# S5 states laid out by step within a chunk, tokens reordered through the gated linear layer

## The chip, the cores and the metric

The kernel runs on one core of one Trainium2 chip. The metric is the device time of one execution in microseconds (us), as the median of several; smaller is better.

## The reference, cut to what matters

One layer of a hybrid decoder for 288 tokens: 256 of one prompt, and 8 sampled sequences of 4 tokens. After a norm, z = a @ w_in is split into an mLSTM part and a part u for the S5 part (64 groups of 16 channels, 64 complex states each). The S5 part is

```python
ab = exp(dt * A)                       # complex, one per group and state
bu = einsum('gpc,bsgc->bsgp', Bb, u)   # complex
st[t] = ab * st[t-1] + bu[t]           # along the tokens of each sequence
y  = einsum(C_re, st_re) - einsum(C_im, st_im) + D * u
ys = gelu(y)
ys = ys * sigmoid(ys @ w_glu + b_glu)  # the gated linear layer, per token
mix = concat(hm, ys) @ w_out
```

`hm` is the mLSTM part's result. The states at the last token of each sequence are outputs too. Behind it come a PEER feed-forward layer (routed experts) and a gated embedding, which the change doesn't touch. Everything is in 32 bits.

## The kernel before, in words

Activations lie with channels on the 128 partitions and the T = 288 tokens along the free dimension: tokens 0 to 255 are the prompt (TP), then sample token TP + 4 b + s for sequence b and step s. A large tile `work` holds, one behind the other, the S5 states `st` (real and imaginary part, each NJ = 32 tiles of 288), `zT` (32 tiles), `uT` (8 tiles), `mix` (16 tiles) and a scratch area. There are 8 PSUM banks `ps`.

Each engine has its own program; they are tied by counting semaphores, and each engine runs its instructions in the order written. The order of the work around the change is by hand:

1. PE, `pe_linear` (L246): the "u" linear, 8 tiles of 128 columns, 16 matmuls over k each, weights streamed by SP through the two halves of `ring`. ACT's `copy_tiles` (L1783, L1792) copies each tile from PSUM to `uT`. Then PE's gate rows (L1686).
2. ACT computes Exp and Sin (L1802 to L1804) for the discretised A; DVE's `dve_s5_setup` (L456, L492 to L514, then L518 to L534) makes the coefficients, and PE transposes them (L1691, L1696, L1712). `a` broadcast over tokens is a stride of 0 in the innermost dimension. L523 to L526 multiply B by such a broadcast; L531 writes runs of 16 with gaps of 16.
3. PE, L1723: the Bu products, 32 tiles x 2 (real, imaginary); ACT (L1816) and DVE (L1871) copy them to `st`.
4. PE goes on with the "z" linear: 32 tiles, 512 matmuls. Beside it DVE runs the S5 scan, `dve_s5_scan` (L563). The prompt is cut into 16 chunks (NCH) of 16 steps (CH). After four squarings of a (`cmul`, L550) come
   - the samples: 4 steps, each one `cmul_add` (L536) on 8 sequences x 32 tiles = 256 elements;
   - a first loop (L585) of 15 trips: step i + 1 of all 16 chunks at once, 32 x 16 = 512 elements a pass;
   - a middle loop (L591) of 15 trips along the chunks' last steps, 32 elements a pass;
   - a third loop (L602) of 15 trips: adds the carried state, times a power of a, to step i of chunks 1 to 15, 32 x 15 = 480 elements a pass, and a `cmul` of 32 elements for the next power.

   One `cmul_add` is 8 passes (L538 to L541, L543, L544, L546, L547); each reads or writes `st` and the contiguous scratch `tS`. In `st` the token is innermost, so step t of all chunks is every 16th element:

```python
chk = [s[:, :, 0:TP].rearrange("p j (k t) -> p t j k", t=CH) for s in st]
smp = [s[:, :, TP:T].rearrange("p j (b s) -> p s j b", s=NS) for s in st]
```

5. L609 to L614 copy the last states to `send` and release PE (`s5_ready`, `send_ready`). PE, L1735: the products of C with the states, 8 tiles u of 4 x 2 matmuls each over 32 columns, moving operand `st[q][:, 4*u+r, :]`. DVE adds D u (L1876), ACT takes Gelu (L1821), both in place in `uT`. PE then transposes the states (L1741, L1743) and broadcasts 8 gate rows (L1752, evacuated at L1828).
6. PE, the "glu" linear: 8 tiles of 8 matmuls, from `uT`. ACT takes the sigmoid of each from PSUM to `gel` (L1844, two buffers) and DVE multiplies by `uT` into `mix[8 + c]` (L1882). Before that DVE works out the mLSTM gate rows (L879 to L915).
7. The mLSTM part (L705 on; DVE L921 on), then the output projection, which reads `mix` split in two parts.

Only SP issues DMAs: the weights of "u", "z" and "glu" (L1591), each half of `ring` as soon as the block before in it is done, then S5 outputs, mLSTM states and w_out tiles.

Of the kernel before, what the change touches and what calls it, by code (L numbers as in the profile page):

```python
# [39 lines left out]
NJ = G * SP_ // P  # L40
CH = 16
NCH = TP // CH
PH, PK, TK = 8, 128, 16
UA = 36
PLE = 256
# [63 lines left out]
def build(nc, ins, outs):  # L109
    ctx = ExitStack()  # L110
    with ctx:
# [68 lines left out]

            return ap.unsqueeze(len(ap.shape)).to_broadcast([*ap.shape, n])

        st = [wk(O_RE, NJ, T), wk(O_IM, NJ, T)]
        zT = wk(O_Z, 32, T)
        uT = wk(O_U, 8, T)
        mix = wk(O_MIX, 16, T)
        xin = wk(O_Z, 3, D)

        Bn = [wk(0, NJ, GC), wk(512, NJ, GC)]
# [373 lines left out]
        def dve_s5_scan(v, o):  # L563
            o.settle()
            v.wait_ge(sem("s0_copied"), 1)
            a = [abT[:, 0, :], abT[:, 1, :]]
            pw = [a16[:, 0, :], a16[:, 1, :]]
            g2 = [a16[:, 2, :], a16[:, 3, :]]

            ts = [t[:, :, 0] for t in tS]  # L570
            cmul(v, o, pw, a, a, ts)
            for _ in range(3):
                cmul(v, o, pw, pw, pw, ts)

            smp = [s[:, :, TP:T].rearrange("p j (b s) -> p s j b", s=NS) for s in st]
            s0 = [s0T[:, q, :].rearrange("p (b j) -> p j b", j=NJ) for q in range(2)]
            aB = [bc(x, NB) for x in a]
            for s in range(NS):
                src = s0 if s == 0 else [x[:, s - 1] for x in smp]
                cmul_add(v, o, [x[:, s] for x in smp], aB, src, [t[:, :, 0:NB] for t in tS])  # L580

            chk = [s[:, :, 0:TP].rearrange("p j (k t) -> p t j k", t=CH) for s in st]
            aC = [bc(x, NCH).unsqueeze(1) for x in a]
            tC = [t.unsqueeze(1) for t in tS]
            with v.Fori(0, CH - 1) as i:  # L585
                o.loop(i, {"dve_own": CMUL})
                cmul_add(v, o, [x[:, ds(i + 1, 1)] for x in chk], aC, [x[:, ds(i, 1)] for x in chk], tC)
                o.leave(CH - 1)

            end = [s[:, :, CH - 1:TP:CH] for s in st]  # L590
            with v.Fori(0, NCH - 1) as i:  # L591
                o.loop(i, {"dve_own": CMUL})
                cmul_add(v, o, [x[:, :, ds(i + 1, 1)] for x in end], [x.unsqueeze(2) for x in pw],
                         [x[:, :, ds(i, 1)] for x in end], [t[:, :, 0:1] for t in tS])
                o.leave(NCH - 1)

            for q in range(2):
                o.do(v.tensor_copy(g2[q], a[q]))
            o.settle()
            n = NCH - 1  # L600
            prev = [x[:, :, 0:n].unsqueeze(1) for x in end]
            with v.Fori(0, CH - 1) as i:  # L602
                o.loop(i, {"dve_own": CMUL + 6})
                cmul_add(v, o, [x[:, ds(i, 1), :, 1:NCH] for x in chk], [bc(x, n).unsqueeze(1) for x in g2], prev,
                         [t[:, :, 0:n].unsqueeze(1) for t in tS])
                cmul(v, o, g2, g2, a, ts)
                o.leave(CH - 1)
            for q in range(2):
                o.do(v.tensor_copy(send[:, q, 0, :], st[q][:, :, TP - 1]))  # L609
                o.do(v.tensor_copy(send[:, q, 1:1 + NB, :],  # L610
                                   st[q][:, :, TP + NS - 1:T:NS].rearrange("p j b -> p b j")))
            o.settle()
            o.do(v.tensor_copy(g2[0], g2[0]), sem("s5_ready"))
            o.do(v.tensor_copy(g2[1], g2[1]), sem("send_ready"))  # L614
# [1047 lines left out]
        def _(pe):  # L1662
# [67 lines left out]
            for u in range(8):  # L1730
                if u >= 2:
                    pe.wait_ge(sem("y_sum"), u - 1)
                for r in range(4):
                    for q in range(2):
                        m = pe.matmul(ps[4 + u % 2][32 * r:32 * r + 32, 0:T], CT[q][:, u, 32 * r:32 * r + 32],  # L1735
                                      st[q][:, 4 * u + r, :], start=(q == 0), stop=(q == 1))
                m.then_inc(sem("y_done"), 1)

            pe.wait_ge(sem("send_ready"), 1)
# [25 lines left out]
        def _(act):  # L1765
# [30 lines left out]
                        one(i, b)  # L1796
                    o.leave(nb // 2)

            copy_tiles("u", uT)
            act.wait_ge(sem("theta_ready"), 1)  # L1800

            o.do(act.activation(r32[0:NJ, 4, :], r32[0:NJ, 2, :], ACT.Exp))  # L1802
# [10 lines left out]
                              ps[4 + g % 4][:, 0:512].rearrange("p (a b) -> p a b", b=P)), sem("bct_copied"))  # L1813
            for j in range(NJ):
                act.wait_ge(sem("bu_done"), 2 * j + 1)
                o.do(act.copy(st[0][:, j, :], ps[4 + 2 * (j % 2)][:, 0:T]), sem("bu_copied0"))  # L1816
            copy_tiles("z", zT)

            for u in range(8):
# [35 lines left out]
        @block.vector  # L1855
        def _(v):
            o = Own(v, sem("dve_own"))
            v.wait_ge(sem("const_ready"), 1)
            for g in range(1, 12, 2):
                i, q = divmod(g, 4)  # L1860
                t0, n = TOK[i]
                v.wait_ge(sem("xt_done"), g + 1)
                o.do(v.tensor_copy(hT[:, 4 * q:4 * q + 4, t0:t0 + n],
                                   ps[g % 4][:, 0:4 * n].rearrange("p (a b) -> p a b", b=n)), sem("xt_copied1"))
            v.wait_ge(sem("vec_copied"), 1)
            v.wait_ge(sem("xt_copied0"), 6)
            dve_norm(v, o, 0)
            dve_s5_setup(v, o)
            for j in range(NJ):
                v.wait_ge(sem("bu_done"), 2 * j + 2)  # L1870
                o.do(v.tensor_copy(st[1][:, j, :], ps[5 + 2 * (j % 2)][:, 0:T]), sem("bu_copied1"))  # L1871
            v.wait_ge(sem("bu_copied0"), NJ)
            dve_s5_scan(v, o)
            for u in range(8):
                v.wait_ge(sem("y_done"), u + 1)
                o.do(v.scalar_tensor_tensor(uT[:, u, :], uT[:, u, :], gv[:, 80 + u:81 + u], ps[4 + u % 2][:, 0:T],  # L1876
                                            ALU.mult, ALU.add), sem("y_sum"))
            dve_gate_rows(v, o)
            base = STREAM["glu"][0]
            for c in range(8):  # L1880
                v.wait_ge(sem("mm_freed"), 2 * base + c + 1)
                o.do(v.tensor_tensor(mix[:, 8 + c, :], uT[:, c, :], gel[:, c % 2, :], ALU.mult), sem("glu_ready"))  # L1882
            dve_mlstm(v, o)

            squares = dve_squares(v, 1, "tile_freed")

            def add(i, c, s):

                v.wait_ge(sem("q_used"), i * 8 + (4 * c + 4))
                h = low[:, ds(i * (2 * T) + c * T, T)]  # L1890
                o.do(v.tensor_tensor(h, h, ps[4 + s][:, 0:T], ALU.add), sem("tile_freed"))
                squares(i, c, s)

            low_parts(v, o, "out", None, add, {"tile_freed": 2}, ahead=True)
            o.settle()
            low_parts(v, o, "wq", None, None, {}, only_first=True)
            dve_norm(v, o, 1, ffn_h, ffn_l)
            dve_peer(v, o)
            dve_tail(v, o)
# [27 lines left out]
```

## Time and profile before

| | |
|---|---|
| time of the runs | median 3019.31 us of 3 (3018.59 to 3023.04) |
| span of the profiled execution, first to last instruction | 3016.9 us |
| its own time beside that | not given apart; the median of the runs lies 2.4 us above the span |
| mean granted TensorE clock | 0.956 |
| share of the span busy | PE 94%, PEld 88%, DVE 57%, ACT 40%, POOL 0% |
| the chain that ended last | PE 78%, DVE 14%, issue 4%, ACT 2% |
| DMA | 389 MB, mean 129 GB/s |

The span is that of one profiled execution. PE is the matmul side of TensorE and PEld its weight loads, which overlap; DVE is VectorE, ACT ScalarE, POOL GpSimd, SP the engine that issues DMAs. A group of instructions is named by its line, engine and operation, with output and inputs by tile names; "idle before" is the time for which its engine stood still just ahead of it, with what ended that. An fp32 matmul has two records. The granted clock is given as a share of 2.4 GHz: 1.00, or 0.50 for 1.2 GHz.

### The profile page before, as it was taken

The page shows a single profiled execution, that of the slowest core. Times are in us where ns is not written, and L with a number is a line of the kernel's source. Part 1 is how long each engine was busy: PE and PEld are TensorE (multiplying, and loading weights), DVE is VectorE, ACT ScalarE, POOL GpSimd, SP SyncE. Part 2 cuts the span into 40 slices and gives each one's busy share as a digit, 9 for nine tenths or more (in the row PEclk, how much of TensorE's full clock was granted, in tenths as well). Part 3 has the DMA queues.
Part 4 walks back from the last instruction along what each step waited for, and adds up shares of the span by engine and source line. Part 5 has one row for each costly group of instructions (what it writes and reads, how often), then busy time and mean ns, then how long its engine had stood idle before and what let it go on. Part 6 is the DMA issues. An engine that isn't in the chain of part 4 may idle for free.

```text
span 3016.9 us, 53624 instructions
## 1 busy us (share of the span) xinstructions
PE 2834.0 (94%) x19564; PEld 2661.5 (88%) x19564; DVE 1717.4 (57%) x3311; ACT 1213.0 (40%) x2023; POOL 2.5 (0%) x18
## 2 busy tenths in 40 slices
PE   8999946899899998799999999999999999999997
PEld 6677734669799997699999999999999999999887
DVE  2289895566658887933333333335555555555466
ACT  1200002213344446944444444444444444444443
POOL 0000000000000000000000000000000000000000
PEclk9799977779899999999999999999999999999999
DMA  6124412226543331033333333344445544444543
GB/s 163 56 91 132 139 56 86 87 84 182 157 133 125 125 129 66 0 125 127 137 125 126 136 127 125 132 151 166 166 167 167 164 155 162 162 166 166 171 112 115
DMA packets 218075, 389.29 MB, mean 129 GB/s; under 512 B 21348, under 2 KB 167396, under 8 KB 200676
## 3 DMA queue, kind: packets, MB, share of 16 engines
q1 hardware_dynamic: 218020, 388.56, 39.0%
q8 instruction: 34, 0.56, 0.1%
q14 instruction: 21, 0.17, 0.0%
HBM read 374.04 MB, written 14.49 MB: 129 GB/s over the span
## 4 chain that ended last, share of the span: by engine, by line
PE 78%; DVE 14%; issue 4%; ACT 2%; DVEq 1%; DMA 0%; ACTq 0%
PE ps L389 11%; PE ps L390 11%; PE ps L391 11%; PE ps L1182 9%; PE ps L1185 9%; PE ps L1181 9%; PE ps L1113 7%; PE ps L261 3%; PE ps L812 1%; PE ps L1723 1%; DVE work L544 1%; DVE work L547 1%; DVE work L539 1%; DVE work L540 1%; DVE work L541 1%
## 5 line engine op out<-in xcount | busy, mean ns | idle before, releaser
L389 PE MATMUL ps<-ffn_h,part_h 128*128 128x288 f32 x2176 | 685.8, 315 | 14.8 <-issue 10.3
L390 PE MATMUL ps<-ffn_l,part_h 128*128 128x288 f32 x2176 | 642.3, 295 | 0.0
L391 PE MATMUL ps<-ffn_h,part_l 128*128 128x288 f32 x2176 | 639.1, 294 | 0.0
L1181 PE MATMUL ps<-act_h,v_high 128*128 128x288 f32 x2048 | 551.8, 295 | 6.1 <-DVE act_l L1418 3.6
L1182 PE MATMUL ps<-act_l,v_high 128*128 128x288 f32 x2048 | 552.2, 295 | 0.0
L1421 DVE TENSOR_TENSOR v_low<-ring,v_high 128x1024 fp32r<-128x1024 f32 x256 | 313.8, 1226 | 372.1 <-ACT v_high L1292 372.1
L1214 ACT CAST part_h<-ps 128x512 fp32r<-128x512 f32 x512 | 299.7, 586 | 466.1 <-PE ps L1113 465.4
L445 DVE TENSOR_TENSOR part_l<-ps,part_h 128x512 fp32r<-128x512 f32 x368 | 254.0, 691 | 404.9 <-ACT part_h L1214 402.4
L389 PEld LDWEIGHTS ps<-ffn_h,part_h 128*128 128x128 f32 x2176 | 409.8, 188 | 18.0 <-issue 16.2
L390 PEld LDWEIGHTS ps<-ffn_l,part_h 128*128 128x128 f32 x2176 | 412.0, 189 | 0.0
L391 PEld LDWEIGHTS ps<-ffn_h,part_l 128*128 128x128 f32 x2176 | 409.7, 188 | 0.0
L1292 ACT CAST v_high<-ring 128x1024 fp32r<-128x1024 f32 x256 | 268.5, 1049 | 346.0 <-PE ps L1185 346.0
L1181 PEld LDWEIGHTS ps<-act_h,v_high 128*128 128x128 f32 x2048 | 384.8, 188 | 6.5 <-DVE low L1433 3.8
L1182 PEld LDWEIGHTS ps<-act_l,v_high 128*128 128x128 f32 x2048 | 385.5, 188 | 0.0
L261 PE MATMUL ps<-low,ring 128*128 128x288 f32 x1280 | 315.8, 411 | 6.5 <-DVE low L308 6.5
L1185 PE MATMUL ps<-act_h,v_low 128*128 128x288 f32 x2048 | 314.3, 295 | 0.0
L261 PEld LDWEIGHTS ps<-low,ring 128*128 128x128 f32 x1280 | 246.2, 193 | 76.4 <-issue 7.7
L1113 PE MATMUL ps<-ident,ring 128*128 128x128 f32 x2048 | 305.9, 272 | 2.0 <-ACT work L1206 1.1
L1185 PEld LDWEIGHTS ps<-act_h,v_low 128*128 128x128 f32 x2048 | 287.0, 188 | 0.0
L1113 PEld LDWEIGHTS ps<-ident,ring 128*128 128x128 f32 x2048 | 250.6, 141 | 2.5 <-ACT work L1206 1.4
L445 DVE TENSOR_TENSOR part_l<-ring,part_h 128x512 fp32r<-128x512 f32 x160 | 108.3, 690 | 95.0 <-ACT part_h L429 94.6
L429 ACT CAST part_h<-ring 128x512 fp32r<-128x512 f32 x160 | 98.4, 620 | 144.5 <-PE ps L391 138.8
(339 smaller groups left out, 3212.2 us busy)
## 6 DMA issues: line engine op xcount, KB each, us to landing
ring<-in_peer_u SPq DMA_DIRECT2D x128, 1024.0 KB, 5.3
ring<-in_peer_v SPq DMA_DIRECT2D x128, 1024.0 KB, 5.6
ring<-in_w_in SPq DMA_DIRECT2D x20, 2048.0 KB, 8.0
ring<-in_w_out SPq DMA_DIRECT2D x16, 1024.0 KB, 5.9
ring<-in_w_ple_gate SPq DMA_DIRECT2D x16, 1024.0 KB, 5.9
out<-work SPq DMA_DIRECT2D x37, 256.0 KB, 3.2
work<-in_state_mlstm_C SPq DMA_DIRECT2D x32, 256.0 KB, 4.9
ring<-in_peer_w_q SPq DMA_DIRECT2D x8, 1024.0 KB, 5.7
```

The costliest lines, as they stand in the source:

```text
L261: m = pe.matmul(ps[2 * s + c][:, 0:T], ring[:, s, k * WB + c * P:k * WB + (c + 1) * P], rhs[:, k, :], start=(k == 0), stop=(k == kt - 1))
L389: pe.matmul(bank, w_h, rhs_h, start=start, stop=False)
L390: pe.matmul(bank, w_h, rhs_l, start=False, stop=False)
L391: return pe.matmul(bank, w_l, rhs_h, start=False, stop=stop)
L445: o.do(v.tensor_tensor(part_l[:, q, :], src, part_h[:, q, :].bitcast(F32), ALU.subtract), sem("low_done"))
L1113: m = pe.transpose(ps[q][:, j * P:(j + 1) * P], natural[s][:, k * P:(k + 1) * P], ident[:])
L1181: pe.matmul(ps[c][:, 0:T], w_h, a_h, start=st_, stop=False)
L1182: pe.matmul(ps[c][:, 0:T], w_h, a_l, start=False, stop=False)
L1185: m = pe.matmul(ps[c][:, 0:T], vl[:, s, c * P:(c + 1) * P], a_h, start=False, stop=sp_)
L1214: o.do(act.copy(part_h[:, q, :], ps[q][:, 0:512]), sem("high_done"))
L1292: o.do(act.copy(vh[:, s % 2, :], natural[s // 2][:, 1024 * (s % 2):1024 * (s % 2) + 1024]), sem("vh_done"))
L1421: o.do(v.tensor_tensor(vl[:, s % 2, :], natural[s // 2][:, 1024 * (s % 2):1024 * (s % 2) + 1024], vh[:, s % 2, :].bitcast(F32), ALU.subtra ...
```

## The change

A new constant CW = 16 + 32/16 = 18 is the number of tokens of one step. `st` becomes (step i of 16, tile j of 32, c of 18): for step i and tile j first the 16 chunks' token of that step, then 2 sample tokens (sample step s and sequence pair m have i = 4 s + m, c = 16 + b mod 2). All of one step's rows now lie in one stretch of 32 x 18 elements, and 16 chunks are neighbours. Neither size nor place of any tile changes.

The tokens of `uT` are put in the order (i, c) too, when ACT copies the u tiles from PSUM: two copies a tile instead of one (prompt, samples), written out instead of looped. They stay in it through Bu, the y products, Gelu and the glu linear, which work per token. L1882's product puts them back in order while it writes `mix`, in two passes a tile instead of one. The Bu copies (L1816, L1871), the passes of the scan, the copies to `send` and L1735's moving operand use the new layout; counts of semaphores, DMAs and matmuls stay.

```diff
--- before.py
+++ after.py
@@ -40,6 +40,7 @@
 NJ = G * SP_ // P
 CH = 16
 NCH = TP // CH
+CW = NCH + NS * NB // CH
 PH, PK, TK = 8, 128, 16
 UA = 36
 PLE = 256
@@ -180,10 +181,21 @@
 
             return ap.unsqueeze(len(ap.shape)).to_broadcast([*ap.shape, n])
 
-        st = [wk(O_RE, NJ, T), wk(O_IM, NJ, T)]
+        st = [work[:, O_RE + q * (O_IM - O_RE):O_RE + q * (O_IM - O_RE) + NJ * T].rearrange("p (i j c) -> p i j c", i=CH, c=CW) for q in range(2)]
         zT = wk(O_Z, 32, T)
         uT = wk(O_U, 8, T)
         mix = wk(O_MIX, 16, T)
+
+        def by_step(ap):
+
+            both = ap.rearrange("p (i c) -> p i c", c=CW)
+            return both[:, :, 0:NCH], both[:, :, NCH:CW].rearrange("p (s m) c -> p s m c", s=NS)
+
+        def by_token(ap):
+
+            return (ap[:, 0:TP].rearrange("p (k i) -> p i k", i=CH),
+                    ap[:, TP:T].rearrange("p (m c s) -> p s m c", s=NS, c=CW - NCH))
+
         xin = wk(O_Z, 3, D)
 
         Bn = [wk(0, NJ, GC), wk(512, NJ, GC)]
@@ -572,14 +584,16 @@
             for _ in range(3):
                 cmul(v, o, pw, pw, pw, ts)
 
-            smp = [s[:, :, TP:T].rearrange("p j (b s) -> p s j b", s=NS) for s in st]
-            s0 = [s0T[:, q, :].rearrange("p (b j) -> p j b", j=NJ) for q in range(2)]
-            aB = [bc(x, NB) for x in a]
+            W2 = CW - NCH
+            smp = [x[:, :, :, NCH:CW].rearrange("p (s m) j c -> p s m j c", s=NS) for x in st]
+            s0 = [s0T[:, q, :].rearrange("p (m c j) -> p m j c", j=NJ, c=W2) for q in range(2)]
+            aB = [bc(x, W2).unsqueeze(1).to_broadcast([P, NB // W2, NJ, W2]) for x in a]
+            tW = [t.rearrange("p j c -> p (j c)")[:, 0:NB * NJ].rearrange("p (m j c) -> p m j c", j=NJ, c=W2) for t in tS]
             for s in range(NS):
                 src = s0 if s == 0 else [x[:, s - 1] for x in smp]
-                cmul_add(v, o, [x[:, s] for x in smp], aB, src, [t[:, :, 0:NB] for t in tS])
-
-            chk = [s[:, :, 0:TP].rearrange("p j (k t) -> p t j k", t=CH) for s in st]
+                cmul_add(v, o, [x[:, s] for x in smp], aB, src, tW)
+
+            chk = [x[:, :, :, 0:NCH] for x in st]
             aC = [bc(x, NCH).unsqueeze(1) for x in a]
             tC = [t.unsqueeze(1) for t in tS]
             with v.Fori(0, CH - 1) as i:
@@ -587,7 +601,7 @@
                 cmul_add(v, o, [x[:, ds(i + 1, 1)] for x in chk], aC, [x[:, ds(i, 1)] for x in chk], tC)
                 o.leave(CH - 1)
 
-            end = [s[:, :, CH - 1:TP:CH] for s in st]
+            end = [x[:, CH - 1, :, 0:NCH] for x in st]
             with v.Fori(0, NCH - 1) as i:
                 o.loop(i, {"dve_own": CMUL})
                 cmul_add(v, o, [x[:, :, ds(i + 1, 1)] for x in end], [x.unsqueeze(2) for x in pw],
@@ -606,9 +620,8 @@
                 cmul(v, o, g2, g2, a, ts)
                 o.leave(CH - 1)
             for q in range(2):
-                o.do(v.tensor_copy(send[:, q, 0, :], st[q][:, :, TP - 1]))
-                o.do(v.tensor_copy(send[:, q, 1:1 + NB, :],
-                                   st[q][:, :, TP + NS - 1:T:NS].rearrange("p j b -> p b j")))
+                o.do(v.tensor_copy(send[:, q, 0, :], st[q][:, CH - 1, :, NCH - 1]))
+                o.do(v.tensor_copy(send[:, q, 1:1 + NB, :].rearrange("p (m c) j -> p m j c", c=W2), smp[q][:, NS - 1]))
             o.settle()
             o.do(v.tensor_copy(g2[0], g2[0]), sem("s5_ready"))
             o.do(v.tensor_copy(g2[1], g2[1]), sem("send_ready"))
@@ -1733,7 +1746,7 @@
                 for r in range(4):
                     for q in range(2):
                         m = pe.matmul(ps[4 + u % 2][32 * r:32 * r + 32, 0:T], CT[q][:, u, 32 * r:32 * r + 32],
-                                      st[q][:, 4 * u + r, :], start=(q == 0), stop=(q == 1))
+                                      st[q][:, :, 4 * u + r, :], start=(q == 0), stop=(q == 1))
                 m.then_inc(sem("y_done"), 1)
 
             pe.wait_ge(sem("send_ready"), 1)
@@ -1796,7 +1809,10 @@
                         one(i, b)
                     o.leave(nb // 2)
 
-            copy_tiles("u", uT)
+            for b in range(8):
+                act.wait_ge(sem("mm_done"), 2 * STREAM["u"][0] + b + 1)
+                for x, (d, e) in enumerate(zip(by_step(uT[:, b, :]), by_token(ps[b % 4][:, 0:T]))):
+                    o.do(act.copy(d, e), sem("mm_freed") if x else None)
             act.wait_ge(sem("theta_ready"), 1)
 
             o.do(act.activation(r32[0:NJ, 4, :], r32[0:NJ, 2, :], ACT.Exp))
@@ -1813,7 +1829,8 @@
                               ps[4 + g % 4][:, 0:512].rearrange("p (a b) -> p a b", b=P)), sem("bct_copied"))
             for j in range(NJ):
                 act.wait_ge(sem("bu_done"), 2 * j + 1)
-                o.do(act.copy(st[0][:, j, :], ps[4 + 2 * (j % 2)][:, 0:T]), sem("bu_copied0"))
+                o.do(act.copy(st[0][:, :, j, :], ps[4 + 2 * (j % 2)][:, 0:T].rearrange("p (i c) -> p i c", c=CW)),
+                     sem("bu_copied0"))
             copy_tiles("z", zT)
 
             for u in range(8):
@@ -1868,7 +1885,8 @@
             dve_s5_setup(v, o)
             for j in range(NJ):
                 v.wait_ge(sem("bu_done"), 2 * j + 2)
-                o.do(v.tensor_copy(st[1][:, j, :], ps[5 + 2 * (j % 2)][:, 0:T]), sem("bu_copied1"))
+                o.do(v.tensor_copy(st[1][:, :, j, :], ps[5 + 2 * (j % 2)][:, 0:T].rearrange("p (i c) -> p i c", c=CW)),
+                     sem("bu_copied1"))
             v.wait_ge(sem("bu_copied0"), NJ)
             dve_s5_scan(v, o)
             for u in range(8):
@@ -1879,7 +1897,9 @@
             base = STREAM["glu"][0]
             for c in range(8):
                 v.wait_ge(sem("mm_freed"), 2 * base + c + 1)
-                o.do(v.tensor_tensor(mix[:, 8 + c, :], uT[:, c, :], gel[:, c % 2, :], ALU.mult), sem("glu_ready"))
+                parts = zip(by_token(mix[:, 8 + c, :]), by_step(uT[:, c, :]), by_step(gel[:, c % 2, :]))
+                for x, (d, y, w) in enumerate(parts):
+                    o.do(v.tensor_tensor(d, y, w, ALU.mult), sem("glu_ready") if x else None)
             dve_mlstm(v, o)
 
             squares = dve_squares(v, 1, "tile_freed")
```

## Rows read from the trace of the kernel before

**Rows 1.** The page, part 1: busy us (share of the span) xinstructions

```profile
PE 2834.0 (94%) x19564; PEld 2661.5 (88%) x19564; DVE 1717.4 (57%) x3311; ACT 1213.0 (40%) x2023; POOL 2.5 (0%) x18
```

**Rows 2.** Waits of PE, 90 to 560 us: in total, times, longest

```profile
PE ps L1735 <- DVE work L613: 64.6, 1, 64.6
PE ps L1712 <- DVE ex L534: 5.6, 1, 5.6
```

**Rows 3.** Timeline: start us, us, engine, line, operation, [idle <-releaser]

```profile
403.71 5.74 PE L261 MATMUL ps<-low,ring 128*128 128x288 f32 x23
...
409.62 0.37 SPq L1591 DMA_DIRECT2D ring<-in_w_glu  x1
...
473.85 0.18 DVE L613 COPY work<-work 128x32 f32<-128x32 f32 x1
...
474.09 9.74 PE L1735 MATMUL ps<-work 128*32 128x288 f32 x128 [64.63 <-DVE work L613]
```

**Rows 4.** Timeline of DVE where the scan begins

```profile
159.05 0.21 DVE L552 TENSOR_TENSOR work<-work 128x32 f32<-128x32 f32 x1 [0.20 <-DVE work L1871]
```

**Rows 5.** Groups of DVE by shape: busy, mean ns; first loop of the scan

```profile
L546 DVE TENSOR_TENSOR work<-work 128x512 f32 x15 | 16.0, 1068 | 0.5
...
L539 DVE TENSOR_TENSOR work<-work 128x512 f32<-128x512 f32 x15 | 15.3, 1019 | 0.0
```

**Rows 6.** The same view, third loop of the scan

```profile
L546 DVE TENSOR_TENSOR work<-work 128x480 f32 x15 | 15.2, 1010 | 0.5
...
L539 DVE TENSOR_TENSOR work<-work 128x480 f32<-128x480 f32 x15 | 14.5, 967 | 0.0
```

**Rows 7.** The same view, passes over other layouts

```profile
L1882 DVE TENSOR_TENSOR work<-work,gel 128x288 f32<-128x288 f32 x8 | 3.5, 454 | 10.7 <-ACT gel L1844 10.7
...
L531 DVE TENSOR_TENSOR work<-work 64x512 f32<-64x512 f32 x4 | 2.7, 687 | 0.1
...
L546 DVE TENSOR_TENSOR work<-work 128x256 f32<-128x256 f32 x4 | 2.5, 628 | 0.1
...
L523 DVE TENSOR_TENSOR work<-work 128x512 f32<-128x512 f32 x1 | 0.7, 692 | 0.1
```

**Rows 8.** The same view, middle loop of the scan

```profile
L538 DVE TENSOR_TENSOR work<-work 128x32 f32<-128x32 f32 x15 | 3.3, 218 | 6.5 <-DVE work L547 6.5
```

**Rows 9.** Timeline from the last u copy to PE's L1691

```profile
93.88 0.40 ACT L1792 COPY work<-ps 128x288 f32 x1 [7.36 <-PE ps L261]
...
96.32 0.28 DVE L492 TENSOR_TENSOR work<-work 32x128 f32<-32x128 f32 x1 [55.53 <-ACT work L1804]
...
101.53 0.32 PEld L1691 LDWEIGHTS ps<-ident,work 32*128 32x128 f32 x4 [0.48 <-DVE work L514]
```

**Rows 10.** Groups by shape: copies from PSUM by ACT and DVE

```profile
L1871 DVE COPY work<-ps 128x288 f32<-128x288 f32 x32 | 14.5, 457 | 36.3 <-PE ps L1723 36.3
L1816 ACT COPY work<-ps 128x288 f32<-128x288 f32 x32 | 12.7, 398 | 30.7 <-PE ps L1723 30.4
...
L1812 ACT COPY work<-ps 128x512 f32<-128x512 f32 x8 | 4.4, 593 | 7.0 <-PE ps L1712 7.0
```

**Rows 11.** Timeline: two successive DVE L1876 behind L1735

```profile
480.96 0.52 DVE L1876 SCALAR_TENSOR_TENSOR work<-work,gv,ps 128x288 f32<-128x288 f32 x1 [0.46 <-PE ps L1735]
...
481.93 0.52 DVE L1876 SCALAR_TENSOR_TENSOR work<-work,gv,ps 128x288 f32<-128x288 f32 x1 [0.46 <-PE ps L1735]
```

**Rows 12.** Windows: us, busy by engine, PE clock, DMA share, GB/s

```profile
380.00:409.00 29.00, 29.00 (x121) 22.75 (x120) 27.08 (x46) 1.19 (x3) 0.00 (x0) 1.00 0.32 107
...
474.00:475.00 1.00, 0.91 (x8) 0.45 (x12) 0.11 (x2) 0.00 (x0) 0.00 (x0) 0.50 0.00 0
480.00:482.00 2.00, 2.00 (x40) 1.47 (x36) 1.09 (x3) 0.90 (x3) 0.00 (x0) 1.00 0.00 0
...
492.00:498.00 6.00, 6.00 (x13) 4.21 (x13) 0.00 (x0) 5.59 (x6) 0.00 (x0) 0.50 0.01 3
```

**Rows 13.** Timeline of DVE behind the last glu product

```profile
545.48 0.17 DVE L921 COPY ex<-ps 128x8 f32<-128x8 f32 x1 [18.10 <-PE ps L728]
```

## The prediction

> **What bounds the kernel now.** I read the page first, then the waits of PE, then the seam that the waits point at, in the timeline. PE is busy for 2834.0 of the 3016.9 us of the span [rows 1], so a change on another engine can only pay where PE stands still for it. Between 90 and 560 us the waits of PE hold one such place: L1735, the product of CT with the S5 states, waits 64.6 us for DVE L613; the next largest wait is 5.6 us [rows 2]. The timeline shows the seam. The last group of the "z" linear starts at 403.71 and lasts 5.74 us, so PE is done at 409.45; DVE is then in the last of its three loops and releases PE only with L613, which starts at 473.85; L1735 begins at 474.09, after 64.63 us of idle PE [rows 3]. The scan started at 159.05 with L552 [rows 4], right behind the last Bu copy, and z behind the last Bu product. So two chains start together near 159 us: PE's z linear, some 250 us, and DVE's scan, 315 us. The scan ends last by 64.6 us, and that is all the change can win from the scan: past it, PE's z linear ends the stage.
>
> Why are the passes of the scan so long? The first loop (L587) runs 15 trips of 8 passes over 128x512, the third (L604) 15 trips of 8 over 128x480. The means of the eight 512 passes lie between 1019 and 1068 ns (the cheapest and the dearest are shown) [rows 5], those of the eight 480 passes between 967 and 1010 ns [rows 6]. The same engine, operation and number of elements takes 692 ns in L523, which also has one operand broadcast along the inner 16, and 687 ns in L531, whose inner runs are 16 elements with gaps between them; 288 elements in L1882 take 454 ns [rows 7]. What L538 to L547 have and these rows lack is an inner step of 16 tokens (64 B). The sample passes, with an inner step of 4 tokens, take 628 ns for 256 elements [rows 7]. From 454 and 692 ns, a contiguous element costs 238/224 = 1.06 ns, so 480 elements cost 692 - 32 x 1.06 = 658 ns and 256 cost 420 ns.
>
> **The change part by part.**
> *Scan loops.* The change gives each step i of the chunk its own block of 32 rows, each of 18 consecutive tokens-by-chunk; a pass reads 16 (or 15) neighbours of each row. I take the contiguous price, since L531's runs of 16 with gaps are nearest in shape. The first loop's passes take (1019 + 1068)/2 = 1044 ns in the middle [rows 5], so 8 x (1044 - 692) = 2.8 us are saved a trip, 42.2 us in 15. The third loop's take 989 ns [rows 6]: 8 x (989 - 658) = 2.65 us a trip, 39.7 us in 15. Together 81.9 us. The bounds: the upper is this; the lower is nothing, if rows at a pitch of 72 B behave like the 64 B steps of today. The middle loop (15 trips of 8 passes of 32 elements) and the cmul of the third loop touch single elements before and after, only at other pitches: L538 at 32 elements takes 218 ns with a pitch of 1152 B, L552 takes 0.21 us with 64 B [rows 4, 8]. So nothing.
> *Sample passes.* 32 passes of 256 elements now have pairs of neighbours in the inner dimension. Between 628 ns (nothing saved) and 420 ns (6.7 us saved) I take nothing; the scan ends early enough either way.
> The scan then ends at 474.1 - 81.9 = 392.2 us, 17 us before PE is done at 409.45 [rows 3]. The wait of 64.6 us goes whole as soon as 64.6/240 = 0.27 us a pass is won of the 0.34 (81.9/240) that I expect. What is late next is PE's own z linear, which the change doesn't touch. **Term: -64.6 us.**
> *u copies on ACT.* Eight copies of 128x288 (0.40 us) become sixteen: 256 elements read at steps of 64 B from PSUM, and 32. Seven of the eight pairs lie beside PE, with some 7 us of idle ACT before each, as before the last (7.36). The last doesn't lie beside it: it starts at 93.88, ACT's Exp and Sin follow, they release DVE L492 at 96.32, DVE's chain ends with L514, and PE L1691 at 101.53 waited its last 0.48 us for that [rows 9]. So what the last pair costs more shifts all of it, z and scan alike. From ACT's 398 ns at 288 and 593 at 512 [rows 10], 0.87 ns an element: 256 cost 370, 32 cost 175, and back to back some 0.1 us overlaps: 0.45 against 0.40, the lower bound +0.05. With DVE's excess of (1040 - 692)/512 = 0.68 ns an element for the step it is 0.62, +0.22; twice that excess gives the upper bound, +0.40. **Term: +0.2 us.**
> Here ACT reads PSUM in steps, which no row of before does. The Trainium skill (SBUF — State Buffer, the paragraph on cachelines) says that PSUM lines hold two fp32 values and that non-contiguous PSUM access slows matmuls; by that rule the copy too should be slower and the term lie nearer to +0.4 than to +0.05. The same paragraph says that an SBUF line is 16 bytes and wants two hits: the 628 ns of the 16 B step [rows 7] agree, and by it the pairs of the sample passes would be at full rate, the scan ending at 385.5 us instead of 392.2. Neither is needed for the sum.
> *Bu copies (L1816, L1871).* 64 copies now write rows of 18 with gaps. They take 398 and 457 ns and wait for PE (30.7 and 36.3 us in total) [rows 10]; PE sets this stage. At nothing; if each rose by a half, still covered, but for the last, +0.2.
> *y matmuls (L1735).* The moving operand becomes 16 rows of 18 instead of 288 in a row. No row of before shows PE reading so. Bounds: nothing, or DVE's ratio 1040/692 = 1.5 on the steady pace of 0.97 us a tile (from one L1876 to the next [rows 11]), 8 x 0.49 = +3.9. I take nothing, since runs of 18 are nearer to L531's than to steps.
> *The clock of L1735.* After the idle stretch the granted clock is 0.50 (the 1.2 GHz level), and is still so at 474 to 475; from 480 on it is 1.00 [rows 12]. The eight tiles take from 474.09 to 483.83; at the steady pace they take 7.8 us. Without the idle stretch PE enters at 1.00 (380 to 409 us shows it) [rows 12]. **Term: -1.9 us.** The clock is down again at 0.50 in 492 to 498, in the first glu tiles, behind the thin broadcasts of L1752 [rows 12]; I keep that as it is. If it doesn't fall, up to 3 us more are won (the 6 us from 492 to 498 at twice the rate); if it falls already as L1735 begins, up to 7.8 are lost.
> *glu products (L1882).* Eight of 454 ns become sixteen: 256 elements written in steps (0.42 to 0.63) and 32 (0.21). At most +0.4 each. The earlier ones lie beside PE's glu tiles, with 10.7 us of idle DVE before them [rows 7]; after the last, DVE idles 18.10 us before L921 [rows 13]. At nothing; were that cover gone, 8 x 0.4 = 3.2 us.
> *Copies to send (L609, L610), waits.* Four copies ahead of L613, in DVE's slack. No DMA is added or moved. SP's glu load of 409.62 starts when z is done [rows 3]; L1735 and L1752 lie before its use, as now. No wait is added; behind L613 nothing stands now that is due before z's end.
>
> **Sum** against the profiled execution: 3016.9 - 64.6 + 0.2 - 1.9 = 2950.6 us of span. The median of the runs is 3019.3, 2.4 us above this span; the execution is an ordinary one. So 2953.0 us.
>
> **Rivals.**
> *A, the cover holds only in part.* The passes fall to some 0.85 us instead of 0.69 because rows of 16 at a 72 B pitch, half of them off a 16 B boundary, are dearer than L531's aligned ones. For: no row has that pitch. Against: L531 and L523 both at 690. Then 240 x 0.18 = 43 us are won, 3019.3 - 43 + 0.2 = 2976; it would have any value from 2953 up to 3019.
> *B, PE reads gapped rows slowly.* L1735 costs up to 3.9 us more: 2957. Against: the runs are long. For: never shown.
> *C, slower.* The place is st: each row start costs extra and the 16 neighbours gain nothing from being neighbours. 32 row starts at the step's excess of 0.68 ns make 22 ns a pass, 240 passes 5.2 us; L1735 then still starts late at half clock and reads at the 1.5 ratio, 9.7 x 0.5 = 4.9; the u copy 0.2: 3019.3 + 10.3 = 3029.6. It decides if a 512 pass measures above about 1.03 us. Against it stand the two rows at 690.
> *D, the step is not what makes the passes slow.* Scan as now, 3019.5.
> *E, clock.* The fall comes at another point between L1735 and glu: 2950 to 2961.
>
> **How the numbers follow.** Main case 0.72, own range 2948 to 2958; A 0.08; B 0.07; E, beyond the main range, 0.06; C 0.02; D 0.02; 0.03 for what I don't see. The range 2946 to 2964 takes in the main case, B, most of E, and the top of A's gain. A measurement of this kernel can tell about 0.2%, 6 us, from no change: faster (0.95) holds main, A, B, E and most of what I don't see; same (0.03) is D and the weak end of A; slower (0.02) is C.
>
> **What would show it.** L538 to L547 at 512 near 690 ns and at 480 near 658; L613 near 392 us or earlier; no wait of L1735 on DVE, its start within 1 us of z's end near 409.7; the clock 1.00 there and L1735 in about 7.8 us; the waits of PE without a new one from glu on. It is wrong if the passes stay above 0.78 us (A, D), if L1735 takes over 9 us at clock 1.00 (B), or if a new PE wait shows between 410 and 480.

## The result and the profile after

The changed kernel takes 2947.8 us in the median of 4 runs (2945.4 to 2953.7), beside 3021.0 us (3018.6 to 3023.0, 4 runs) for the kernel before: a ratio of 0.9762, 95% interval 0.9749 to 0.9776. Forecast were 2953.0 us in a range of 2946 to 2964, and faster. The span of the profiled execution is 2945.5 us, against 3016.9. Lines of the new kernel are 12 or more higher: its L550 to L559 are L538 to L547 of before, L626 is L613, L1748 is L1735, L1765 is L1752.

The three longest waits of PE between 90 and 500 us, to be held against [rows 2]; the columns are total, times, longest.

```profile
PE ps L1725 <- DVE ex L546: 5.6, 1, 5.6
PE ps L741 <- ACT low L853: 4.9, 1, 4.9
PE ps L1765 <- ACT work L1842: 1.4, 1, 1.4
```

The wait of 64.6 us is gone and no new one stands in its place. The seam, where z ends and the y products begin, is in the timeline as follows (before: [rows 3]):

```profile
386.61 0.18 DVE L626 COPY work<-work 128x32 f32<-128x32 f32 x1
...
409.73 8.04 PE L1748 MATMUL ps<-work 128*32 128x288 f32 x128
```

DVE now releases PE at 386.8 and PE comes for it only at 409.73, when z is done. The row of PE carries no bracket: nothing was waited for. The distance between the two, the cover, is 22.9 us. The groups of DVE by shape (busy, mean ns; before: [rows 5], [rows 6] and the sample passes of [rows 7]):

```profile
L558 DVE TENSOR_TENSOR work<-work 128x512 f32 x15 | 10.4, 693 | 0.5
...
L551 DVE TENSOR_TENSOR work<-work 128x512 f32<-128x512 f32 x15 | 10.3, 683 | 0.0
...
L558 DVE TENSOR_TENSOR work<-work 128x480 f32 x15 | 9.9, 659 | 0.5
...
L553 DVE TENSOR_TENSOR work<-work 128x480 f32<-128x480 f32 x15 | 9.8, 650 | 0.0
...
L1902 DVE TENSOR_TENSOR work<-work,gel 128x256 f32<-128x256 f32 x8 | 4.6, 591 | 9.4 <-ACT gel L1861 9.2
...
L558 DVE TENSOR_TENSOR work<-work 128x256 f32<-128x256 f32 x4 | 1.7, 426 | 0.1
```

The dearest and the cheapest of each kind of loop pass stand here; all are at the contiguous price now, the sample passes (last row) too. Only the glu product that writes in steps (L1902) takes 591 ns for 256 elements. ACT's u copies, and the last pair of them in the timeline (before: [rows 9]):

```profile
L1815 ACT COPY work<-ps 128x256 f32<-128x256 f32 x8 | 3.0, 376 | 65.5 <-PE ps L273 65.5
...
L1815 ACT COPY work<-ps 128x32 f32<-128x32 f32 x8 | 1.6, 194 | 0.0
```

```profile
94.09 0.46 ACT L1815 COPY work<-ps 128x256 f32<-128x256 f32 x2 [7.29 <-PE ps L273]
```

In windows (the last three columns are granted clock, DMA share, GB/s; before: [rows 12]):

```profile
405.00:410.00 5.00, 5.00 (x25) 3.60 (x26) 0.00 (x0) 0.06 (x1) 0.00 (x0) 1.00 0.00 0
412.00:414.00 2.00, 2.00 (x40) 1.44 (x36) 1.09 (x3) 0.98 (x3) 0.00 (x0) 1.00 1.07 375
422.00:424.00 2.00, 2.00 (x9) 1.37 (x7) 0.00 (x0) 1.61 (x5) 0.00 (x0) 0.84 0.00 0
424.00:430.00 6.00, 6.00 (x14) 3.95 (x13) 0.00 (x0) 5.28 (x6) 0.00 (x0) 0.50 0.01 3
```

PE enters the y products at 1.00, and its clock falls to 0.50 only near 423.4, in the broadcasts of L1765. Those broadcasts before and after:

```profile
485.94 6.26 PE L1752 MATMUL ps<-ex,ident 8*128 8x288 f32 x16 [1.35 <-ACT work L1825]
```

```profile
419.88 4.67 PE L1765 MATMUL ps<-ex,ident 8*128 8x288 f32 x16 [1.35 <-ACT work L1842]
```

**Where the 71.4 us of span went.** Milestones on PE, before and after: y products start 474.09 and 409.73 (-64.4); they take 9.74 and 8.04 us (-1.7); the broadcasts take 6.26 and 4.67 (-1.6), since the clock fell about 2 us into them before and about 3.5 us now; so glu starts 67.6 us earlier, 492.13 and 424.48. The output projection starts 67.9 us earlier (681.3 and 613.4), the first product of the PEER layer does (803.4 and 735.5), and so does the second expert product (2029.7 and 1961.8). That product and the tail give 3.5 us more, all of it in code that the change leaves alone. 1.5 us come inside the product, around a wait that both kernels have, and 2.0 behind it; at both places the granted clock was higher after (0.72 and 0.77 over the group behind the product). The stretch of the product that holds the wait, and the first long group behind the product, before and then after:

```profile
2400.00:2600.00 200.00, 196.44 (x1471) 196.24 (x1471) 102.29 (x130) 87.55 (x123) 0.00 (x0) 0.99 0.47 160
```

```profile
2857.40 11.02 PE L220 MATMUL ps<-low,ones 128*128 128x288 f32 x32 [1.85 <-ACT low L278]
```

```profile
2332.10:2532.10 200.00, 196.44 (x1483) 196.24 (x1483) 102.41 (x131) 88.78 (x124) 0.00 (x0) 1.00 0.48 162
```

```profile
2787.41 10.39 PE L232 MATMUL ps<-low,ones 128*128 128x288 f32 x32 [1.85 <-ACT low L290]
```

Nothing ties these 3.5 us to the change. From the first glu product to the end the profiled execution took 2524.8 us before and 2521.1 after; in the ones of the experiments below it took 2519.7 to 2526.0, and in that of experiment 1, which enters glu within 0.1 us of the changed kernel, 2524.8 again.

### The profile page after: what moved, and what is told of

Its sections match the earlier page's. It is cut to its first block, busy times and chain, and to the rows that moved or that the text cites. A ratio compares the mean times of both kernels' runs of the same rounds, so it can differ in the third digit from the quotient of the medians.

```text
span 2945.5 us, 53619 instructions
## 1 busy us (share of the span) xinstructions
PE 2826.0 (96%) x19564; PEld 2656.0 (90%) x19564; DVE 1629.2 (55%) x3319; ACT 1214.6 (41%) x2031; POOL 2.5 (0%) x18
## 4 chain that ended last, share of the span: by engine, by line
PE 73%; DVE 7%; issue 1%; ACT 1%; DVEq 0%; DMA 0%; ACTq 0%
PE ps L401 12%; PE ps L402 11%; PE ps L403 11%; PE ps L1195 9%; PE ps L1198 9%; PE ps L1194 9%; PE ps L1126 7%; PE ps L825 1%; PE ps L767 1%; DVE ring L1397 1%; DVE ring L1393 1%; DVE part_l L1325 1%; DVE rstd L337 0%; DVE work L1405 0%; PE ps L1495 0%
```

## The experiments

**1. Which distance makes a pass long.** The changed kernel with extra passes in idle stretches, behind the scan on DVE and ahead of the z copies on ACT; results go to dead scratch or back to where they were read.

```diff
+            tt = lambda d, x, y: o.do(v.tensor_tensor(d, x, y, ALU.max))
...
+            tt(d5, c5, fl[:, 0:1024:2])
...
+            tt(D3, C3, r16)
...
+            tt(d5.rearrange("p (a b) -> p a b", b=2), c5.rearrange("p (a b) -> p a b", b=2),
+               fl[:, 0:4096].rearrange("p (a b) -> p a b", b=16)[:, :, 0:2])
...
+               fl[:, 0:4096].rearrange("p (a b) -> p a b", b=16)[:, :, 3:5])
...
+            tt(bt[:, 0:2048:4], c5, c5)
...
+            o.do(act.copy(s3(sa[:, 0:256]), tr(sp_)))
```

Here `d5`, `D3`, `c5` and `C3` are contiguous scratch and `fl` is the start of `work`. `r16` takes every 16th element of it. The other passes have the same form with other steps.

> The changed kernel with passes of other layouts added in idle stretches: 13 DVE maxima of 512 elements and 4 copies of 256 between the scan and the copies to send (some 13 us, all before z's end at 409.7), and 7 ACT copies of 256 elements ahead of the z copies. Theory 1 (a pass is slow when successive elements lie apart by more than some distance, whatever the 16-byte lines): contiguous and runs of 16 take 0.69 us, steps of 8, 16, 32 and 64 B from some step on all take about 1.02 us, pairs of neighbours with gaps about 0.85, at either alignment alike. Theory 2 (16-byte lines, as the Trainium skill's page SBUF - State Buffer states it): steps of 8 B and runs of 2 inside a line or of 4 take 0.69, steps of 16, 32 and 64 B take 1.02, and pairs that straddle a line boundary take 1.02 too. ACT: if the 0.46 us of the u copies mean that ACT does not mind steps, all seven copies take 0.37 us; if only PSUM reads are free of it, those that read or write SBUF in steps take 0.5 or more. The kernel's time stays that of the changed one, 2948 +- 3 us.

The DVE passes in the timeline, each 512 elements. In order: runs of 16 with gaps; step 8 B; step 16 B; step 64 B; pairs at 0 and 1 of every 16 elements; pairs at 3 and 4; runs of 4; two reads and the write in steps of 64 B; a write in steps of 16 B; a write in steps of 8 B.

```profile
386.58 0.69 DVE L631 TENSOR_TENSOR work<-work 128x512 f32<-128x512 f32 x1
...
387.30 0.69 DVE L631 TENSOR_TENSOR work<-work 128x512 f32<-128x512 f32 x1
...
388.03 1.10 DVE L631 TENSOR_TENSOR work<-work 128x512 f32<-128x512 f32 x1
...
390.28 1.04 DVE L631 TENSOR_TENSOR work<-work 128x512 f32<-128x512 f32 x1
...
391.35 0.69 DVE L631 TENSOR_TENSOR work<-work 128x512 f32<-128x512 f32 x1
...
392.08 1.05 DVE L631 TENSOR_TENSOR work<-work 128x512 f32<-128x512 f32 x1
...
393.17 0.69 DVE L631 TENSOR_TENSOR work<-work 128x512 f32<-128x512 f32 x1
...
394.99 1.10 DVE L631 TENSOR_TENSOR work<-work 128x512 f32<-128x512 f32 x1
...
396.13 1.10 DVE L631 TENSOR_TENSOR work<-work 128x512 f32<-128x512 f32 x1
...
397.26 0.69 DVE L631 TENSOR_TENSOR work<-work 128x512 f32<-128x512 f32 x1
```

Theory 2 holds at each point, and Theory 1 falls. The two rows of pairs decide: same count, same pitch of 64 B, 0.69 us for elements 0 and 1, 1.05 us for elements 3 and 4, which lie on either side of a multiple of 16 B. A step of 16 B is as dear as one of 64. A read and a write in steps of 16 B cost alike (1.10 each). In steps of 64 B one read costs 1.04, and two reads and the write together hardly more (1.10). That is the rule of the Trainium skill (SBUF — State Buffer, the paragraph on cachelines: a 16-byte line wants two accesses in succession); the ten passes shown agree with it.

The copies, 256 elements each: first DVE from PSUM in order and in steps of 64 B, and from SBUF in order and in steps; then ACT from PSUM in order, in steps; from SBUF in order, in steps.

```profile
397.99 0.43 DVE L662 COPY work<-ps 128x256 f32<-128x256 f32 x1
398.45 0.42 DVE L664 COPY work<-ps 128x256 f32<-128x256 f32 x1
398.90 0.29 DVE L666 COPY work<-work 128x256 f32<-128x256 f32 x1
399.23 0.38 DVE L668 COPY work<-work 128x256 f32<-128x256 f32 x1
```

```profile
158.78 0.37 ACT L1889 COPY work<-ps 128x256 f32<-128x256 f32 x1 [0.27 <-PE ps L1784]
159.19 0.37 ACT L1891 COPY work<-ps 128x256 f32<-128x256 f32 x1
159.59 0.40 ACT L1893 COPY work<-work 128x256 f32<-128x256 f32 x1
160.03 0.62 ACT L1895 COPY work<-work 128x256 f32<-128x256 f32 x1
```

Reading PSUM in steps of 64 B costs neither engine anything; reading SBUF in steps costs ACT 0.22 us and DVE 0.09 at 256 elements. So the change puts its permutation on the free side when it reads u out of PSUM. The kernel as a whole took 2950.9 us in its one run, within the spread of the changed kernel: 14 us of work on DVE were covered.

**2 and 3. The cover, and what an idle stretch costs.** The changed kernel with 39, then 69, contiguous passes between scan and `send` (13 rounds of 3, and 23 rounds in experiment 3).

```diff
+            for _ in range(13):
+                o.settle()
+                for x in tS[1:4]:
+                    o.do(v.tensor_tensor(x, tS[0], tS[0], ALU.max))
+            o.settle()
```

> 39 contiguous DVE passes of 512 elements between the scan and the copies to send, about 25 us, into a slack that the trace puts at 22.9 us. If the cover is as the trace has it: PE waits 2 to 4 us before the y matmuls, the clock stays 1.00 through them, and the time rises by 2 to 4 us over the changed kernel's 2948. Rival (the end of the scan still matters before z's end): the time rises by about 25 us.

> 69 such passes, about 45 us. PE waits about 22 us before the y matmuls, the granted clock falls to 0.50 in that wait, the y matmuls take 9.7 us instead of 8.0, and the time rises by 22 us for the wait and about 1.7 for the clock: about 2972. If the idle stretch did not set the clock there, they take 8.0.

39 passes (25.0 us): 2950.0 us, span 2948.3, 2.8 more than the changed kernel. 69 passes: 2972.5 us, span 2970.7, 25.2 more. Each is a single run, beside which the kernel before took 3014.3 us and not 3021.0, so a few us in these totals can't be told; the seam in the traces can. The waits and the y products in the two timelines:

```profile
411.44 9.73 PE L1753 MATMUL ps<-work 128*32 128x288 f32 x128 [2.21 <-DVE work L631]
```

```profile
432.97 10.68 PE L1753 MATMUL ps<-work 128*32 128x288 f32 x128 [21.63 <-DVE work L631]
```

The cover is as the trace had it: 25.0 us into 22.9 leave a wait of 2.2. (The y products start only 1.7 us later than at 409.73, since this execution came to its first Bu product 0.6 us sooner, at 114.51 and not 115.08.) One part of the expectation of experiment 2 missed: I expected the clock to stay at 1.00 over so short a wait. It did not:

```profile
412.00:414.00 2.00, 2.00 (x28) 1.11 (x21) 0.51 (x1) 0.44 (x1) 0.00 (x0) 0.62 0.91 320
414.00:416.00 2.00, 2.00 (x24) 0.95 (x17) 0.51 (x1) 0.44 (x1) 0.00 (x0) 0.53 0.04 8
```

PE waited for 2.2 us, and from about 412.5 to 415.9 it ran at 0.50, so the y products took 9.73 us instead of 8.04. The price doesn't follow the length of the wait: behind 2.2, 6.8, 9.7, 21.6 and 64.6 us (experiments 2, 9, 6, 3 and the kernel before) the y products took 9.73, 10.76, 9.72, 10.68 and 9.74 us. At this seam an idle stretch costs its own length and 1.7 to 2.7 us of clock on top.

**4. Is the gain capped by z?** The kernel before, its layout untouched, with the whole third loop left out: the carried states are not added to the steps.

```diff
-            n = NCH - 1
-            prev = [x[:, :, 0:n].unsqueeze(1) for x in end]
-            with v.Fori(0, CH - 1) as i:
...
-                o.leave(CH - 1)
```

> The kernel before with the third loop of the scan left out (the carried states are not added to the steps of each chunk), its layout unchanged. The scan is some 134 us shorter and ends near 340 us. Theory (the gain is capped by z's end): PE's wait goes, L1735 starts near 409.5, the time is that of the changed kernel, 2948 +- 4. Rival (the stage is as long as its scan): 3017 - 134 = 2883. If the new layout itself helped PE or what follows, this kernel would stay some us above the changed one.

It took 2946.7 us in its one run, span 2945.0. Its scan releases PE at 340.1 us, 46 us before the changed kernel's, and it is not faster:

```profile
339.97 0.18 DVE L605 COPY work<-work 128x32 f32<-128x32 f32 x1
...
409.32 8.04 PE L1727 MATMUL ps<-work 128*32 128x288 f32 x128
```

So past z's end a shorter scan is worth nothing. From the first Bu product to the first y product it takes 294.65 us, as the changed kernel does to the hundredth (359.37 in the kernel before). The new layout does nothing else for the kernel either: this one has the old one, and the same span to 0.5 us.

**5. Is the detour through glu needed?** `st` laid out as in the change, but u, Gelu and glu in token order; the Bu copies and the y sums permute.

```diff
-                for x, (d, e) in enumerate(zip(by_step(uT[:, b, :]), by_token(ps[b % 4][:, 0:T]))):
-                    o.do(act.copy(d, e), sem("mm_freed") if x else None)
+                o.do(act.copy(uT[:, b, :], ps[b % 4][:, 0:T]), sem("mm_freed"))
...
+                for x, (d, e) in enumerate(zip(st_parts(0, j), by_token(ps[4 + 2 * (j % 2)][:, 0:T]))):
+                    o.do(act.copy(d, e), sem("bu_copied0") if x else None)
```

> The changed kernel without the reordering of tokens in u, Gelu and glu: u, its copies and the glu products stay in order; the 64 Bu copies read PSUM in steps (two copies a tile, 128 in all) and the y sums read it in the new order and write u in steps (two passes a tile). Theory (the reordering through the glu layer costs and gains almost nothing, since its extra passes are covered): the scan passes stay at 0.69 us, PE's pace of 1.33 us a Bu tile covers the split copies (0.55 to 0.65 us), and the y sums at 0.59 + 0.21 us a tile against 0.52 slow the y products a little, 0 to 2 us; the time is 0 to +3 us against the changed kernel. Rival (the split copies come late for PE's two buffers in the Bu stage): up to 32 x 0.3 = +10 us.

2953.7 us (2949.0 to 2958.4, 4 runs), ratio to the kernel before 0.9791 (0.9774 to 0.9808). The changed kernel stood at 0.9762 (0.9749 to 0.9776) in its first 4 runs and at 0.9781 (0.9767 to 0.9794) beside experiment 8 below. Beside the second figure the difference can't be told from nothing; beside the first it is some 9 us, with intervals that just overlap. In the experiment's trace PE waits nowhere new in the Bu stage, the split copies (424 + 180 ns on DVE) are covered, and the y products take 8.80 us instead of 8.04: the y sums are now 676 ns for 256 elements, since they read and write u in steps. So the rival's wait in the Bu stage didn't come. Glu starts at 427.15 instead of 424.48; besides the y products, the broadcasts behind them took 6.51 us instead of 4.67, as the clock fell sooner. Whether the detour brings that too is not shown; what it saves for certain is 0.8 us at L1748.

**6. PE ends the stage; can it be shorter?** With 22.9 us of slack on DVE, the stage is PE's, and its dearest stretch is this one, the Bu products of the changed kernel at half clock:

```profile
130.00:150.00 20.00, 20.00 (x57) 12.80 (x56) 6.15 (x15) 5.61 (x14) 0.00 (x0) 0.50 0.00 1
```

I put 2 matmuls of z behind every Bu pair, for the first 4 of z's 32 tiles.

```diff
+                b, k = j // 8, 2 * (j % 8)
...
+                for kk in (k, k + 1):
+                    m = pe.matmul(ps[b][:, 0:T], ring[:, b // 2, kk * WB + (b % 2) * P:kk * WB + (b % 2 + 1) * P],
+                                  nT[:, kk, :], start=(kk == 0), stop=(kk == KD - 1))
```

> The changed kernel with the first 4 of 32 z tiles taken into the Bu stage on PE: behind each of the 32 Bu pairs two z matmuls. In the changed kernel the Bu stage takes 40 us at a granted clock of 0.50 although PE is busy, and DVE has 22.9 us of slack. Theory (the thin Bu matmuls, 32 of 128 rows, let the clock fall; z matmuls between them keep it up): the stage with 4 z tiles takes 31 + 21 = 52 us instead of 40 + 31 = 71, z ends some 15 to 19 us earlier near 392; the scan starts 12 us later and ends near 399, so it is again what ends last: a wait of PE of about 7 us, and the time falls by 9 to 11 us against the changed kernel. Rival (the clock falls all the same): the stage takes some 40 + 55 us with half rate z tiles, the scan starts later by 55 us, and the time rises by 20 us or more.

```profile
130.00:150.00 20.00, 20.00 (x70) 11.39 (x68) 3.66 (x8) 3.78 (x10) 0.00 (x0) 1.00 0.00 1
```

```profile
159.51 1.24 PE L1741 MATMUL ps<-low,ring 128*128 128x288 f32 x4
...
160.68 1.23 PE L1735 MATMUL ps<-work 32*128 32x288 f32 x4
...
161.84 1.24 PE L1741 MATMUL ps<-low,ring 128*128 128x288 f32 x4
```

The clock stayed at 1.00, as the theory had it. (The short waits for the Bu copies, 0.63 and 0.28 us ahead of the fall in the changed kernel, are gone here as well; this run can't tell whether they or the thin products let the clock fall.) The time didn't follow: 2957.7 us (2955.7 to 2961.3). A step of one pair and two z matmuls takes 2.33 us, of which each half is 1.16 us from start to start, although 4 records of z take 0.97 in a row; the 32 steps are 75 us, not 52. The scan starts at 192.9 instead of 159.3, ends at 420.2, and PE waits 9.7 us. My estimate took the parts at their undisturbed pace and left out what a change of shape costs. On the side of z that is 0.2 us a change, and the lumps of 8 and 16 records in experiments 8 and 9 show the same (2.13 us instead of 1.94, 4.08 instead of 3.88). On the side of Bu the loss is larger: two pairs in a row, on different row groups, take 1.25 us, and a pair by itself takes 1.16. How much of this is the change of shape and how much the missing neighbour no run separates.

**7 to 9. Larger lumps.** The changed kernel again, and z matmuls behind every 4 pairs: 4 of them (2 tiles of z), or 8 (4 tiles). The lines shown are those of experiment 8; in experiment 9 they read `8 * (j // 4)` and `k + 8`.

```diff
+                if j % 4 < 3:
+                    continue
+                b, k = divmod(4 * (j // 4), KD)
...
+                for kk in range(k, k + 4):
```

> The changed kernel itself, beside the next two on one chip: 2948 +- 3 us. The spread of its runs shows how much of a difference can be told.

> The changed kernel with the first 2 of 32 z tiles taken into the Bu stage, 4 z matmuls behind every 4 Bu pairs (the version with 2 z matmuls behind every single pair kept the clock at 1.00 but took 2.33 us a step, since each switch between 32-row and 128-row matmuls costs PE some 0.2 to 0.4 us). Theory (the Bu stage is held by its clock, and z work in larger lumps keeps that up with a quarter of the switches): 4 pairs in 3.7 us at the pace that the stage has before its clock falls (0.93 a pair), 4 z matmuls in 1.9 and 0.4 for the switches make 6.0 us, 48 in all against 40 + 15.5; z ends 7 us earlier, the scan starts 8 us later and ends near 395, still covered; the time falls by 7 us against the changed kernel. Rival (with so little z work between them the clock falls in the Bu pairs as now): the stage takes at least 40 + 15.5 us, more where z runs at half rate, and the time rises by 0 to 15 us.

> As e8, with the first 4 z tiles, 8 z matmuls behind every 4 Bu pairs. Theory: 3.7 + 3.9 + 0.4 = 8.0 us a step, 64 in all against 71: z ends 7 us earlier, near 403; the scan starts 24 us later and ends near 411, so PE waits 8 us and the clock falls in that wait (1.7): the time rises by 1 to 4 us against the changed kernel, although PE's work is the shorter one. Rival (the clock falls in the Bu pairs): the stage takes 71 us or more and the time rises by 12 us or more.

| | median us (5 runs) | ratio to before, 95% interval |
|---|---|---|
| the changed kernel | 2951.2 (2947.2 to 2954.9) | 0.9781 (0.9767 to 0.9794) |
| 2 tiles of z in lumps of 4 | 2942.0 (2939.7 to 2945.2) | 0.9745 (0.9732 to 0.9759) |
| 4 tiles of z in lumps of 8 | 2945.3 (2941.9 to 2949.1) | 0.9764 (0.9750 to 0.9778) |

The first version beats both kernels: 9 us below the changed one at the medians, with intervals that don't meet. The second lies 6 below it, but its interval overlaps. Their y products:

```profile
401.72 8.04 PE L1760 MATMUL ps<-work 128*32 128x288 f32 x128
```

```profile
402.29 10.76 PE L1760 MATMUL ps<-work 128*32 128x288 f32 x128 [6.83 <-DVE work L628]
```

In the first, z ends 8.0 us earlier and the scan is ready at 393.2 (forecast: 7 and 395). The clock isn't kept up throughout: it is 1.00 from 116 to 130 us, 0.72 in the mean from 130 to 140, 0.94 and 0.75 in the next two stretches of 10. But it is 1.00 when the long row of z matmuls begins, where in the changed kernel it stays at 0.50 for some 5.4 us more.

The profiled executions reach the first Bu product between 113.5 and 118.7 us, so the fair measure is from the first Bu product to the first y product. It is 294.65 us in the changed kernel (both profiles), 285.2 in the first version, 288.8 in the second, and 301.6 in experiment 6. That is 9.5 and 5.8 us less and 7.0 more, and the medians say 9.2, 5.9 and (beside 2951.2) 6.5.

In the second, PE's stage is shorter still, but the scan is what ends last, with a wait of 6.8 us and the clock's price behind it. I had forecast a loss of 1 to 4 us there, with the scan starting 24 us later and ready at 411; it started 15.5 us later and was ready at 402.1. The steps took what was forecast (64.6 us for all, and not 64). What was wrong is that I let the scan wait for the last lump of z, 4 us, which lies behind the last Bu pair, and took today's stage for 40 us when it takes 43.5; the rest is that this execution reached the stage 1.6 us sooner.

## Why the prediction was right, point by point

- **What bounds the kernel.** Right: one wait of 64.6 us, capped by z's end. The trace after shows the gain of 64.4 us at that seam, experiment 4 shows the cap, experiment 2 the cover.
- **Scan loops.** 692 and 658 ns were forecast, 683 to 693 and 650 to 659 measured. DVE's release was put at 392.2 us, or 385.5 if the pairs of the sample passes were at full rate; it came at 386.8, with 418 to 426 ns for those passes. The scan as a whole went from 315.0 to 227.5 us. For the sample passes I had taken no gain; the full-rate price was the right one. It cost the forecast nothing, as it lies under the cover.
- **u copies.** The mechanism (only the last pair counts) is right, the size was not: +0.2 forecast on DVE's excess for steps, +0.06 measured (0.46 against 0.40 us), at the lower bound. The Trainium skill's sentence on PSUM lines (SBUF — State Buffer, the paragraph on cachelines) speaks of matmuls; carried over to copies, as I did, it pointed to +0.4, and the traces don't agree for copies on ACT or DVE (experiment 1). For matmuls no run here shows it.
- **y matmuls.** Nothing was forecast for the 16 rows of 18, and nothing it is: experiment 4 reads 288 in a row, and both take 8.04 us. Rival B falls.
- **The clock of L1735.** -1.9 forecast, -1.7 measured. I kept the later fall as it was; it came later, which gave 1.6 us more (within the bound of 3 us that I had named). So rival E's mechanism took part, on its fast side.
- **Bu copies, glu products.** Covered, as forecast: the Bu copies keep 401 and 457 ns; L1902 takes 591 and 210 ns a tile, and DVE idles 17.9 us behind the last.
- **Rivals A, C and D** fall with the passes at 690 ns. Rival A's mechanism, rows off a 16 B boundary, is not a made-up one: experiment 1 shows it for pairs. In rows of 15 or 16 at a pitch of 72 B at most one element of a row stands alone within its 16 B.
- **The sum.** 66.3 us were forecast, the profile shows 71.4, the medians of the runs 73.2. The missing 5 us are the 1.6 at the broadcasts and the 3.5 of the last product and the tail, both at stretches where the granted clock happened to be higher. The 1.6 came again in experiments 1, 4 and 7 (broadcasts of 4.57 to 4.74 us), though not in 5 and 8, which have no wait at the seam either (6.51 and 5.65); the 3.5 were gone again in experiment 1. With them 2947.8 lies just below the range of 2948 to 2958 that I had given the main case, and only 1.8 above the lower end of the whole range: the mechanism was right, and the 5 us by which the total is off lie in the clock, where no term of the sum foresaw them. That the total still fell inside the range owes something to luck. The runs of the changed kernel spread over 8 us (2947 to 2955 in experiment 7, with mean clocks of 0.968 to 0.966), so a part of a few us is not told better than that.

## What to carry to other kernels

Where two engines run side by side, a faster pass pays up to the other engine's end and no further: read that distance first, here 64.6 us of the 87.5 that the scan lost. Lay operands out so that two neighbours within 16 B are used in succession, and do unavoidable permutations on the read from PSUM, where they were free. Once the cover has turned into slack, spend it: work of the critical engine moved under the slack, in lumps, gave another 9 us. Count the slack against the lumps too: twice as many z matmuls used it up and gave no more.

## What the runs showed that I had not expected

- A pause of 2.2 us on PE was enough to bring its clock from 1.00 down to 0.50 for some 3.4 us, at a price of 1.7 us in the next 8 us of work (experiment 2).
- ACT and DVE copies read PSUM in steps of 64 B at the price of contiguous ones (0.37 and 0.37, 0.43 and 0.42 us), but ACT pays 0.62 instead of 0.40 for the same from SBUF.
- A change between the Bu shape (32 rows) and the full shape cost a lump of z 0.2 us, whether it had 4, 8 or 16 records (experiments 6, 8 and 9), and a single Bu pair between z matmuls took 1.16 us where two in a row take 1.25. With 32 such steps a gain became a loss of 7 us (experiment 6).
